# Feed-forward gate and up products as seven block products in place of eight, with the operand sums on GpSimd

## What is computed

```python
def swiglu(x, w_gu, w_down):
    gate, up = jnp.split(x @ w_gu, 2, axis=-1)
    return (jax.nn.silu(gate) * up) @ w_down

x = x + 0.5 * swiglu(rms_norm(x, p['ffn1_norm']), p['ffn1_w_gu'], p['ffn1_w_down'])
...
x = x + 0.5 * swiglu(rms_norm(x, p['ffn2_norm']), p['ffn2_w_gu'], p['ffn2_w_down'])
```

## Time and profile before

| what | value |
| --- | --- |
| three timed runs | 1570.07, 1571.0, 1579.16 us (median 1571.0) |
| span of the profiled execution | 1570.0 us |
| busy in it | PE 1477.6, PEld 1332.4, DVE 662.6, ACT 494.3, POOL 78.7 us |
| chain that ended last | PE 86%, DVE 9%, ACT 2%, issue 1%, DMA 1% |
| first feed-forward block | 0 to 487 us, of it gate/up 21.8 to 337.4 |
| mixer | 487 to 1091 us |
| second feed-forward block | 1091 to 1570 us, of it gate/up 1099.8 to 1416 |

### The profile page before, as it was taken

How to read it: one execution, slowest core, us unless ns; L and a number is a source line. 1 busy time by engine, 2 the same in 40 slices (tenths; PEclk the granted TensorE clock), 3 DMA queues, 4 the chain that set the end, 5 groups by cost and what they waited for, 6 DMA issues and landing times.

```text
span 1570.0 us, 23071 instructions
## 1 busy us (share of the span) xinstructions
PE 1477.6 (94%) x9189; PEld 1332.4 (85%) x9189; DVE 662.6 (42%) x1115; ACT 494.3 (31%) x865; POOL 78.7 (5%) x74
## 2 busy tenths in 40 slices
PE   5999999999997999999989988688999999999999
PEld 5999999998886998787877665476999999998887
DVE  4222122224446666647645666635312222124444
ACT  5212122123335453533243332433311212113332
POOL 0000000000000000212022221000000000000000
PEclk9999999999998999999997999899999999999999
DMA  6322222233100422101030025660322222406000
GB/s 189 103 57 78 80 80 73 74 144 124 27 0 18 144 67 85 54 28 54 36 114 1 1 76 190 233 213 1 81 81 80 80 60 74 120 0 254 0 34 33
DMA packets 139312, 127.20 MB, mean 81 GB/s; under 512 B 3845, under 2 KB 107909, under 8 KB 139260
## 3 DMA queue, kind: packets, MB, share of 16 engines
q1 hardware_dynamic: 136748, 117.15, 24.0%
q0 software_dynamic: 2512, 9.34, 1.7%
HBM read 115.83 MB, written 10.39 MB: 80 GB/s over the span
## 4 chain that ended last, share of the span: by engine, by line
PE 86%; DVE 9%; ACT 2%; issue 1%; DMA 1%; POOL 0%; SPq 0%; DVEq 0%; ACTq 0%
PE psum_all L514 25%; PE psum_all L515 24%; PE psum_all L516 24%; PE psum_all L1421 2%; PE psum_all L1668 1%; PE psum_all L1434 1%; DVE hT_lo L329 1%; PE psum_all L1671 1%; PE psum_all L1537 1%; DVE x_norm L296 1%; PE psum_all L1426 1%; DMA K_c<-cache_k 0%; PE psum_all L342 0%; PE psum_all L1794 0%; DMA x_tok<-x_prompt 0%
## 5 line engine op out<-in xcount | busy, mean ns | idle before, releaser
L514 PE MATMUL psum_all<-hT_hi,gu_hi 128*128 128x320 f32 x1408 | 438.3, 311 | 8.8 <-DVE hT_lo L329 8.8
L515 PE MATMUL psum_all<-hT_lo,gu_hi 128*128 128x320 f32 x1408 | 437.6, 311 | 0.0
L516 PE MATMUL psum_all<-hT_hi,gu_lo 128*128 128x320 f32 x1408 | 437.5, 311 | 0.0
L514 PEld LDWEIGHTS psum_all<-hT_hi,gu_hi 128*128 128x128 f32 x1408 | 267.2, 190 | 9.7 <-issue 6.1
L516 PEld LDWEIGHTS psum_all<-hT_hi,gu_lo 128*128 128x128 f32 x1408 | 267.1, 190 | 0.0
L515 PEld LDWEIGHTS psum_all<-hT_lo,gu_hi 128*128 128x128 f32 x1408 | 267.1, 190 | 0.0
L466 DVE TENSOR_TENSOR aT<-silu_gate,psum_all 128x320 f32 (+1 forms) x88 | 39.0, 484 | 462.6 <-PE psum_all L516 462.6
L514 PE MATMUL psum_all<-wd_hi,a_hi 128*128 128x512 f32 x440 | 171.8, 390 | 1.9 <-DVE x_tok L509 1.7
L515 PE MATMUL psum_all<-wd_lo,a_hi 128*128 128x512 f32 x440 | 171.4, 390 | 0.0
L516 PE MATMUL psum_all<-wd_hi,a_lo 128*128 128x512 f32 x440 | 171.4, 389 | 0.0
L391 ACT ACTIVATE gu_hi<-raw_gu 128x1024 fp32r<-128x1024 f32 x88 | 88.4, 1052 | 245.7 <-PE psum_all L516 245.7
(11 more groups left out here) (306 smaller groups left out, 1951.3 us busy)
## 6 DMA issues: line engine op xcount, KB each, us to landing
raw_gu<-ffn_w_gu SPq DMA_DIRECT2D x88, 512.0 KB, 5.0
wd<-ffn_w_down SPq DMA_DIRECT2D x8, 2048.0 KB, 14.9
raw_b<-w_in SPq DMA_DIRECT2D x8, 1024.0 KB, 5.1
K_c<-cache_k SPq DMA_DIRECT2D x8, 1024.0 KB, 8.6
V_c<-cache_v SPq DMA_DIRECT2D x8, 1024.0 KB, 5.5
raw_cv<-w_in SPq DMA_DIRECT2D x13, 512.0 KB, 3.9
wd<-ffn_w_down SPq DMA_DIRECT2D x4, 1024.0 KB, 10.2
x_mid<-x_tok SPq DMA_DIRECT2D x1, 2048.0 KB, 10.3
```

The costliest lines, as they stand in the source:

```text
L514: nc.tensor.matmul(out, lhs_hi, rhs_hi, start=start, stop=False, skip_group_check=True)
L515: nc.tensor.matmul(out, lhs_hi, rhs_lo, start=False, stop=False, skip_group_check=True)
L516: return nc.tensor.matmul(out, lhs_lo, rhs_hi, start=False, stop=stop, skip_group_check=True)
```

## The change

For a unit the two 128-column blocks (gate, up) and the two halves of the depth (512 each) form a 2x2 block matrix, and the depth halves with two sets of tokens (the first and the second 64 of each tile) another. Their product takes seven block products (Strassen's identity in Winograd's form) in place of eight. Each product is 4 blocks in depth by 320 tokens, three matmuls each: 12 matmuls, so 84 in a unit. For that:

- `ffn_pool` (new): GpSimd makes four sums of 512 columns of the raw weights for each unit (`sums`), three of them in place, and once for each tile four sums of 256 columns of the transposed norm (`token_sums`).
- The weights are rounded and subtracted in seven operands of 512 columns for each unit (`operand_act`, `operand_dve`, one buffer each; before, four instructions in all of 1024). Operand i of unit j+1 is written after product i of unit j.
- The norm's transposes are copied out of PSUM as they are (`h_copy`, `hsum`), then rounded and subtracted as seven blocks `hB_hi`, `hB_lo`: three after the copies, four after the sums (`h_hi`, `h_lo`).
- The outputs are combined outside PSUM: ScalarE copies two products (`p1`, `p5`), VectorE makes four sums (`u2`, `u3`, the odd and the even half), and the two multiplications; before, two multiplications alone.
- The products of three banks are accumulated on after such a copy, so TensorE waits for ScalarE or VectorE before products 3, 4 and 5, and for its operand before each product.
- Unit 0 again goes in two parts (192 and 128 columns). The third tile's transposes stand after the second product of the first part, the fourth's after the fifth. In the first block the operands of unit 0 are made within the norm; in the second, `wout_act` and `wout_dve` make them, one for each of the last seven weight steps of the mixer's output product.
- Memory is laid out anew; the down weights that are loaded before the last gate/up matmul serve four steps, and the next chunk (six steps, 1.5 MB) is issued after the last product.

The core of the diff:

```diff
+        OPS = 7
+        SLOT_OF = (0, 1, 2, 0, 1, 2, 3)
+        H_OF = (0, 4, 3, 1, 5, 2, 6)
+        OPENS = (True, True, True, False, False, False, True)
+        SUM_OF = (None, 3, 2, None, 1, 4, None)
...
+            sp.wait_ge(*s.lo(OPS))
+            ffn_raw(sp, s, w_gu, 2, 0)
+            sp.wait_ge(*s.n.xn(TT))
+            load_down(0, 0)
+            sp.wait_ge(*s.lo(2 * OPS))
+            ffn_raw(sp, s, w_gu, 3, 1)
+            with sp.Fori(2, FT // 2) as pair:
                 j = 2 * pair
                 for slot in range(2):
-                    sp.wait_ge(*s.lo(2 * (j + slot) - 2))
-                    load(j + slot, slot)
-            load_down(0, 0)
+                    sp.wait_ge(*s.lo(OPS * (j + slot - 1)))
+                    ffn_raw(sp, s, w_gu, j + slot, slot)
+            sp.wait_ge(*s.product(FT - 1, 6))
             load_down(0, 1)
-            sp.wait_ge(*s.mm(2 * FT))
+            sp.wait_ge(*s.a(2 * FT))
             load_down(0, 2)
-            load_down(0, 3)
             load_down(1, 0)
             load_down(1, 1)
-            sp.wait_ge(*s.a(2 * FT))
             load_down(1, 2)
...
+        def ffn_pool(pool, s, early=False):
+
+            def sums(j, slot, which):
+                r = raw_gu[slot]
+                A11, A12, A21, A22 = r[:, 0, 0:4], r[:, 0, 4:8], r[:, 1, 0:4], r[:, 1, 4:8]
+                n = 4 * j
+                if 0 in which:
+                    pool.wait_ge(*s.w[slot](16 * (j - slot) + 32))
+                    if not isinstance(j, int) or j:
+                        pool.wait_ge(*s.lo(OPS * (j - 1) + 5))
+                    nc.gpsimd.tensor_tensor(s3[:], A11, A21, ALU.subtract).then_inc(s.sums.sem, 1)
+                    pool.wait_ge(*s.sums(n + 1))
+                    nc.gpsimd.tensor_tensor(A21, A21, A22, ALU.add).then_inc(s.sums.sem, 1)
+                if 1 in which:
+                    pool.wait_ge(*s.sums(n + 2))
+                    pool.wait_ge(*s.lo(OPS * j + 1))
+                    nc.gpsimd.tensor_tensor(A11, A21, A11, ALU.subtract).then_inc(s.sums.sem, 1)
+                    pool.wait_ge(*s.sums(n + 3))
+                    pool.wait_ge(*s.lo(OPS * j + 4))
+                    nc.gpsimd.tensor_tensor(A12, A12, A11, ALU.subtract).then_inc(s.sums.sem, 1)
+
+            def token_sums(t):
+                b11, b21, b22, t1, t2, t3, t4, b12 = (hsum[:, t % 2, i] for i in range(8))
+                pool.wait_ge(*s.cp(2 * t + 2))
+                nc.gpsimd.tensor_tensor(t1, b12, b11, ALU.subtract).then_inc(s.ts.sem, 1)
+                nc.gpsimd.tensor_tensor(t3, b22, b12, ALU.subtract).then_inc(s.ts.sem, 1)
+                pool.wait_ge(*s.ts(4 * t + 1))
+                nc.gpsimd.tensor_tensor(t2, b22, t1, ALU.subtract).then_inc(s.ts.sem, 1)
+                pool.wait_ge(*s.ts(4 * t + 3))
+                nc.gpsimd.tensor_tensor(t4, t2, b21, ALU.subtract).then_inc(s.ts.sem, 1)
+
+            if early:
+                sums(0, 0, (0, 1))
+            token_sums(0)
+            token_sums(1)
+            if not early:
+                sums(0, 0, (0,))
+            token_sums(2)
+            if not early:
+                sums(0, 0, (1,))
+            token_sums(3)
+            token_sums(4)
+            sums(1, 1, (0, 1))
+            with pool.Fori(1, FT // 2) as pair:
+                for slot in range(2):
+                    sums(2 * pair + slot, slot, (0, 1))
...
+        def operand_act(act, s, j, i, slot):
+
+            if i == 0:
+                act.wait_ge(*s.w[slot](16 * (j - slot) + 32))
+            if SUM_OF[i]:
+                act.wait_ge(*s.sums(4 * j + SUM_OF[i]))
+            nc.scalar.activation(gq_hi[i][:], operand(slot, i), ACT.Copy).then_inc(s.hi.sem, 1)
...
+        def operand_dve(dve, s, j, i, slot):
+            dve.wait_ge(*s.hi(OPS * j + i + 1))
+            nc.vector.tensor_tensor(gq_lo[i][:], operand(slot, i), raw(gq_hi[i][:]), ALU.subtract)\
+                .then_inc(s.lo.sem, 1)
...
+        H_SPLIT = (slice(0, 3), slice(3, 7))
...
+            h_copy(act, s, 0)
+            h_hi(act, s, 0, 0)
+            h_copy(act, s, 1)
+            h_hi(act, s, 0, 1)
+            h_hi(act, s, 1, 0)
+            h_copy(act, s, 2)
+            h_hi(act, s, 1, 1)
+            h_hi(act, s, 2, 0)
+            if not early:
+                operand_act(act, s, 0, 0, 0)
+            h_hi(act, s, 2, 1)
+            if not early:
+                for i in range(1, OPS):
+                    operand_act(act, s, 0, i, 0)
+            square(3)
+            square(4)
+            root(3)
+            root(4)
+            copy_p1(act, s, 0, 0, 0)
+            copy_p5(act, s, 0, 0, 0)
+            h_copy(act, s, 3)
+            h_hi(act, s, 3, 0)
+            h_copy(act, s, 4)
+            h_hi(act, s, 3, 1)
+            h_hi(act, s, 4, 0)
+            h_hi(act, s, 4, 1)
...
+            scale(0)
+            inverse(2)
+            scale(1)
+            h_lo(dve, s, 0, 0)
+            scale(2)
+            h_lo(dve, s, 0, 1)
+            h_lo(dve, s, 1, 0)
+            residual(3)
+            h_lo(dve, s, 1, 1)
+            residual(4)
+            h_lo(dve, s, 2, 0)
+            if not early:
+                operand_dve(dve, s, 0, 0, 0)
+            h_lo(dve, s, 2, 1)
+            if not early:
+                for i in range(1, OPS):
+                    operand_dve(dve, s, 0, i, 0)
+            inverse(3)
+            scale(3)
+            inverse(4)
+            scale(4)
+            sum_u2(dve, s, 0, 0, 0)
+            for part in range(2):
+                h_lo(dve, s, 3, part)
+            for part in range(2):
+                h_lo(dve, s, 4, part)
...
+            def unit(j, slot, part=None, last=False):
+                def split(i):
+                    if not last:
+                        act.wait_ge(*s.product(j, i))
+                        operand_act(act, s, j + 1, i, 1 - slot)
+
+                copy_p1(act, s, j, slot, part)
+                split(0)
+                split(1)
+                if last:
+                    act.wait_ge(*s.lo(OPS * FT))
+                    act.wait_ge(*s.wd[0](16))
+                    down_split_act(act, s, 0, 0, 0, 0)
+                copy_p5(act, s, j, slot, part)
+                split(2)
+                act.wait_ge(*s.product(j, 3))
+                if part is None:
+                    act.wait_ge(*s.a(2 * j))
+                nc.scalar.activation(silu_gate[:], psum[4 * slot][:, 0:HALF], ACT.Silu)\
+                    .then_inc(s.cop.sem, 1)
+                split(3)
+                split(4)
+                if last:
+                    down_split_act(act, s, 0, 0, 1, 1)
+                split(5)
+                act.wait_ge(*s.vec(5 * j + 5))
+                nc.scalar.activation(u2[:], u2[:], ACT.Silu).then_inc(s.cop.sem, 1)
+                split(6)
...
+            def unit(j, slot, part=None, last=False):
+                b = 4 * slot
+
+                def split(i):
+                    if not last:
+                        operand_dve(dve, s, j + 1, i, 1 - slot)
+
+                even, odd = (halves(aT[:, j, :])[:, h] for h in range(2))
+                split(0)
+                sum_u2(dve, s, j, slot, part)
+                if last:
+                    down_split_dve(dve, s, 0, 0, 0, 0)
+                split(1)
+                split(2)
+                split(3)
+                dve.wait_ge(*s.product(j, 4))
+                dve.wait_ge(*s.vec(5 * j + 2))
+                nc.vector.tensor_tensor(u3[:], psum[b + 1][:, 0:HALF], p1[:], ALU.add)\
+                    .then_inc(s.vec.sem, 1)
+                split(4)
+                dve.wait_ge(*s.vec(5 * j + 3))
+                dve.wait_ge(*s.cop(4 * j + 4))
+                nc.vector.tensor_tensor(odd, by_tile(u3[:]), by_tile(p5[:]), ALU.add)\
+                    .then_inc(s.vec.sem, 1)
+                if last:
+                    down_split_dve(dve, s, 0, 0, 1, 1)
+                dve.wait_ge(*s.product(j, 5))
+                dve.wait_ge(*s.vec(5 * j + 2))
+                nc.vector.tensor_tensor(u2[:], u2[:], psum[b + 2][:, 0:HALF], ALU.add)\
+                    .then_inc(s.vec.sem, 1)
+                split(5)
+                dve.wait_ge(*s.product(j, 6))
+                nc.vector.tensor_tensor(even, by_tile(u3[:]), by_tile(psum[b + 3][:, 0:HALF]),
+                                        ALU.subtract).then_inc(s.vec.sem, 1)
+                dve.wait_ge(*s.cop(4 * j + 6))
+                dve.wait_ge(*s.vec(5 * j + 4))
+                nc.vector.tensor_tensor(odd, by_tile(u2[:]), odd, ALU.mult).then_inc(s.a.sem, 1)
+                split(6)
+                dve.wait_ge(*s.vec(5 * j + 6))
+                nc.vector.tensor_tensor(even, by_tile(silu_gate[:]), even, ALU.mult)\
+                    .then_inc(s.a.sem, 1)
...
+            def product(slot, i, cols=slice(0, HALF)):
+                for k in range(KT // 2):
+                    last = three(psum[4 * slot + SLOT_OF[i]][:, cols], gq_hi[i][:, k, :],
```

(31 more changed lines are left out.)

434 lines of the change are left out of this document (245 added, 189 removed).

## The result

The changed kernel takes 1561.3 us (median of 7 runs, 1558.8 to 1563.8) where the kernel before takes 1570.5 beside it: a ratio of 0.994 with a 95% interval of 0.992 to 0.996. So the change gains 9 to 15 us, near the 1% that counts here as no change; 35 were forecast. The profiled execution's span is 1562.0 us.

A forecast was written before the change was run, and what follows sets the result against it. TensorE's matmuls were taken to bound gate/up units, the norm's chain the block starts. 1570.0 - 74.3 (units) + 22 and 14 (starts) + 2 (down product) = 1533.7, plus 1 for the median: 1535 us, range 1510 to 1570.

The forecast's parts named there:

- The gain: Gate/up units: 84 matmuls in place of 96, 12.32 us a unit in place of 14.09, saving 74.3 us.
- Does a unit fit: Other engines' work for a gate/up unit fits into 12.32 us; VectorE needs 11.5 if shut out by all four sums.
- The first rival: VectorE bounds a gate/up unit if a GpSimd sum shuts it out over 1.3 us: 1563 to 1602 us, chance 0.22.
- The chain of the start: Block starts: copies, GpSimd sums, rounding and subtraction, one tile behind the other, 4 to 4.5 us a tile.
- Six products of 128 columns, 72 x 0.1 = 7.2: Last part of unit 0: its 72 matmuls cost 0.1 us each, so unit 0 ends near 1134 in the second block.
- Some 3 us at the slow pace: Unit 0's first part: allowance added to 60 matmuls of 192 columns at about 0.11 us, plus the transposes.
- The start of the first block: First block: unit 0 ends some 64 us after the start, 22 us longer than before; bounds 11 and 30.
- 14 + 8: First block's start: 14 us as in the second block, plus 8 for making unit 0's operands in the same chain.
- The down product: Its next 1.5 MB of weights may come late: 0 to 3.5 us a block, taken as 1.
- The mixer: Seven operands made in its output product's steps, with over 2 us to spare on both engines, cost nothing.
- The cheap start: Rival: sums and subtractions slip past each other, block starts cost 11 and 7 us: 1517 us, chance 0.2.
- the identity that brings nothing: Rival: waits and short accumulations stretch a gate/up matmul to 0.168 us, only costs stay: 1609 us, chance 0.05.

The follow-up runs named there:

- redo: Changed kernel with unit 0's second part taking all 320 columns instead of the last 128, part 1's results thrown away: 1547.6 us, ratio 0.986.
- warm without gaps: Changed kernel with eight and six unused 192-column matmuls filling TensorE's gaps ahead of the first and second products of unit 0's part 2: 1539.0 us, 0.980.
- one row: Changed kernel with unit 0 unsplit and all five tiles going through squares, scaling, transposes and sums one behind the other: 1527.1 us, 0.973.
- one part: Changed kernel with unit 0 unsplit at 320 columns, transposes of tiles 3 and 4 ahead of all products: 1543.0 us, 0.982.
- both moves: Changed kernel with every second down step's rounded hidden units at another SBUF address, 1557.3 us; then the rounded down weights moved as well, 1558.7 us.

## Why the prediction was right and wrong

- **The gain: right.** Forecast 12.32 us a unit, 12.25 measured (12.32 as the mean of a block's 21, since unit 1 begins at the slow pace), no gap of TensorE from unit 1 on. The ten waits a unit cost nothing, as the down product's rows had said.
- **Does a unit fit: right, and as narrowly as worked out, but with luck in the number.** VectorE's need was put at 7.1 us of its own and 4.4 of turns lost to four sums, 11.5; where VectorE's loop sets the pace it is 11.6. But of these VectorE is busy for 9.6, so the turns cost it some 2.5, and the other 2.0 are its waits for roundings, most of it behind the third sum, which the forecast had not counted as VectorE's time. The first rival decides at 0.65 us of reserve, and the run with a sum in the gap crosses that. `p5` and `u2` were named as the tightest waits, and the two runs with more sums stopped at just these. That VectorE is busy 77% says nothing of its reserve.
- **The chain of the start: right to 2.5 us.** In the second block, counted from the first transposes, part 2's second product could begin after 33.6 us by the forecast; it began after 36.1 (1094.95 to 1131.04). Sums were put at 0.65 alone, and take 0.73; 4.2 us a tile, and take 4.4.
- **What failed: "Six products of 128 columns, 72 x 0.1 = 7.2".** They took 15.4. No row stood behind the price of 0.1 us; the forecast had gone down with the columns, from 0.1467 us for 320 to about 0.11 for 192. But the matmul costs 0.111 us for 192 and for 128. And it was a price at the fast clock. "Some 3 us at the slow pace" had been allowed for the whole of part 1 and nothing for part 2, from rows of the slow pace in the start of the kernel before, where 18 and 20 matmuls of 320 columns ran slow before the clock rose. Behind a gap, 72 of 128 columns did not bring it up. That is 8.2 us a block, 16 in all, shown by redo and by warm without gaps; with that term the forecast would have been 1551. The floor at the fast clock fits the Trainium skill ("TensorE: Matmul & The Clock Gate", section "LDWEIGHTS (loading the stationary operand)"): a weight load's time goes by the columns of the weights, which by its formula is an estimate of 0.107 us for 128, beside 0.111 measured. Every matmul here loads new weights, and fewer streamed columns leave that load as it is. No run changed the weight load, so that it is the floor is argued and not shown.
- **The start of the first block.** The 14 + 8 were right in kind: 64 was forecast, 74.4 came, of which 8.2 are part 2's pace. The order that leaves GpSimd idle for 10 us between tiles 2 and 3 was seen in the forecast and priced in its 14; it is worth 9 and 6 us in the two blocks, by the difference of one row to one part.
- **The down product: +1 forecast a block, 2.3 and 2.7 measured.** The forecast's reason was a wait for weights, and no such wait shows; the extra is the steps' 3.51 us, of open cause.
- **The mixer: 0 forecast, +4.1 measured in one profile, -1.9 in the other.** It varies so from execution to execution.

So of the 28 us by which the profile misses the forecast, 16 are part 2's products, 4 to 5 the chain of the starts, 3 the down product and 4 the mixer. 1561 lies inside the range of 1510 to 1570, but by luck: the range reached so far for the first rival's sake, and that one did not come true, though the reserve against it is only 5%. The cheap start and the identity that brings nothing fell both.

## What to carry to other kernels

Splitting a matmul so that its first half can start early is free only while the pieces are not too narrow to get cheaper (here 192 columns cost as much as 128) and TensorE does not wait in between: behind a gap, price the pieces at the slow clock, and ask which later work will bring it up. When a chain over several engines has to be run for each tile, run all tiles through it in one row before anything that can wait. And find an engine's reserve from how fast it goes where it, with the waits of its loop, is the bound (here 11.6 of 12.25 us), not from its busy share.

## What the runs showed of the hardware that was not expected

- At 1.2 GHz 72 matmuls of 128 columns back to back, 15.4 us, did not bring the clock up; 2.8 us of 320-column matmuls behind them did, and so did matmuls of 192 columns in part 1, which start as far apart. At 2.4 GHz the same 72, with no gap ahead, kept it.
- A matmul with new weights takes 0.111 us for 128 and for 192 columns at the fast clock, 0.213 at the slow one.
- Matmuls of 512 columns run 0.228 or 0.234 us apart at clock 1.00, in the down product in turn by step, in the places of the operands before and after both moves.
- In a loop of VectorE, GpSimd and ScalarE, four sums of GpSimd lengthened VectorE's unit from 7.1 us of work to 11.6: some 2.5 by lost turns, 2.0 by waits, most of them for what comes of one sum.
